# Mixture of experts on Trainium2: the gather and the yield change places between large and small experts, and the last layer norm is shared by three engines

## The reference, cut to what matters

```python
logits = (h @ router).astype(F32)
top_val, top_idx = lax.top_k(logits, TOP_K)            # TOP_K = 2
weights = jax.nn.softmax(top_val, axis=-1)
combine = einsum('blk,blke->ble', weights, one_hot(top_idx, N_EXPERTS))
out = 0
for e in range(N_EXPERTS):                             # 8
    gate, up = jnp.split(h @ w13[e], 2, axis=-1)       # 1024 -> 2 x 3584
    out = out + combine[..., e:e+1] * ((silu(gate) * up) @ w2[e])   # 3584 -> 1024
hx = layer_norm(ALPHA * hx + g2x * out, ln_g, ln_b)    # (256, 1024), mean and variance per token
```

## Time and profile before

| | |
|---|---|
| median of 3 runs | 2219.43 us (2217.98 to 2220.53) |
| the profiled execution, its own time | 2225.52 us |
| its span, first to last instruction | 2223.7 us |
| mean granted clock of TensorE | 0.991 |
| TensorE busy | 2137.1 us, 96% of the span |
| VectorE, ScalarE, GpSimd busy | 1176.0, 915.8, 182.7 us |
| expert stage | about 1308 (first load) to 2210 us |
| one couple, from one to the next at the same place | 217.6 us |
| first large expert: its first low digits, its first product | 1339.40, 1342.88 us |
| last small expert: TensorE's idle time ahead of the first down half of chunk 2 | 1.83 us |
| stores of the result issued | 2216.23 us and about 2220.7 us |

### The profile page before, as it was taken

How to read it: one execution, slowest core, us unless ns; L and a number is a source line. 1 busy time by engine, 2 the same in 40 slices (tenths; PEclk the granted TensorE clock), 3 DMA queues, 4 the chain that set the end, 5 groups by cost and what they waited for, 6 DMA issues and landing times.

```text
span 2223.7 us, 56103 instructions
## 1 busy us (share of the span) xinstructions
PE 2137.1 (96%) x24686; PEld 1580.2 (71%) x24686; DVE 1176.0 (53%) x1581; ACT 915.8 (41%) x1200; POOL 182.7 (8%) x185
## 2 busy tenths in 40 slices
PE   8999999899999989999999999999999899989997
PEld 4677668688888747888888868953895399449843
DVE  3544695522233386666666539820982198129802
ACT  3422013522222185555555437711771277027700
POOL 2100372100000002200000110000000000000000
PEclk8999999999999999999999999999999999999999
DMA  8466406333322351111111249999999999999996
GB/s 294 156 224 236 162 1 189 114 95 94 95 96 98 101 156 35 35 35 35 35 35 59 66 181 347 367 367 407 406 407 401 406 407 407 401 407 407 407 391 274
DMA packets 220597, 491.19 MB, mean 221 GB/s; under 512 B 14631, under 2 KB 107711, under 8 KB 220095
## 3 DMA queue, kind: packets, MB, share of 16 engines
q1 hardware_dynamic: 218974, 482.44, 58.4%
q10 hardware_dynamic: 1442, 6.06, 0.8%
HBM read 486.37 MB, written 2.10 MB: 220 GB/s over the span
## 4 chain that ended last, share of the span: by engine, by line
PE 80%; SPq 5%; DMA 5%; DVE 5%; ACT 3%; issue 2%; POOL 1%; DVEq 0%; ACTq 0%; POOLq 0%
PE bank L1821 13%; PE bank L1852 7%; SPq L935 5%; PE bank L1906 4%; DMA expert_w<-in_moe_w_dram 4%; PE bank L1261 4%; PE bank L1262 4%; PE bank L1263 4%; PE bank L1138 2%; PE bank L1429 2%; PE bank L1167 2%; PE bank L1393 2%; PE bank L1139 2%; PE bank L1140 2%; PE bank L1278 2%
## 5 line engine op out<-in xcount | busy, mean ns | idle before, releaser
L3303 DVE TENSOR_TENSOR w_low<-expert_w,w_high 128x1792 fp32r<-128x1792 f32 (+1 forms) x192 | 383.7, 2023 | 42.1 <-ACT w_high L2470 40.3
L2470 ACT CAST w_high<-expert_w 128x1792 fp32r<-128x1792 f32 (+1 forms) x192 | 325.2, 1701 | 104.7 <-PE bank L1821 72.7
L1906 PE MATMUL bank<-expert_w,arena 128*64 128x448 f32 x1024 | 199.1, 541 | 5.2 <-DMA expert_w<-in_moe_w_dram 5.2
L1906 PEld LDWEIGHTS bank<-expert_w,arena 128*64 128x64 f32 x1024 | 72.2, 137 | 121.6 <-issue 120.2
L1821 PE MATMUL bank<-w_high,xg_high 128*128 128x448 f32 x512 | 146.4, 367 | 7.0 <-DVE xg_low L3293 6.4
L1821 PE MATMUL bank<-w_low,xg_high 128*128 128x448 f32 x512 | 144.9, 364 | 0.0
L1821 PE MATMUL bank<-w_high,xg_low 128*128 128x448 f32 x512 | 144.1, 363 | 0.0
L1261 PE MATMUL bank<-u_high,ring_high 128*128 128x512 f32 x352 | 138.6, 394 | 1.9 <-DVE u_low L2943 1.8
L1262 PE MATMUL bank<-u_low,ring_high 128*128 128x512 f32 x352 | 138.0, 392 | 0.0
L1263 PE MATMUL bank<-u_high,ring_low 128*128 128x512 f32 x352 | 137.7, 391 | 0.0
L2517 ACT ACTIVATE arena<-bank 128x448 f32<-128x448 f32 x16 | 8.7, 545 | 259.9 <-PE bank L1906 259.9
(11 more groups left out here) (458 smaller groups left out, 4191.1 us busy)
## 6 DMA issues: line engine op xcount, KB each, us to landing
expert_w<-in_moe_w_dram SPq DMA_DIRECT2D x128, 1792.0 KB, 19.4
expert_w<-in_moe_w_dram SPq DMA_DIRECT2D x32, 2048.0 KB, 19.4
arena<-in_mod_w_dram SPq DMA_DIRECT2D x48, 1024.0 KB, 8.3
expert_w<-in_moe_w_dram SPq DMA_DIRECT2D x32, 1536.0 KB, 19.2
arena<-in_ffn_w_dram SPq DMA_DIRECT2D x44, 512.0 KB, 5.1
arena<-in_hy_w_in_dram SPq DMA_DIRECT2D x12, 1024.0 KB, 5.3
arena<-in_rw_w_rkv_dram SPq DMA_DIRECT2D x48, 256.0 KB, 2.9
arena<-in_ffn_w_dram SPq DMA_DIRECT2D x11, 1024.0 KB, 4.8
```

What stands on the lines that cost most here:

```text
L1906: last = pe.matmul(b[hd(v), 0:EH], small_x[:, k, :], w[:, kk, v * EH:v * EH + EH], start=(k == 0), stop=(k == KT - 1))
L2470: act.copy(high_piece(kind, n), piece(kind, ering[q % ERN], n // 2, n % 2))\
L3303: dve.tensor_tensor(piece(kind, low[s], n // 2, n % 2), piece(kind, ering[s], n // 2, n % 2), high_piece(kind, n).bitcast(F32), ALU.subtract)\
```

## The change

The gather of a large expert becomes that expert's own first step on TensorE (`large_gathered`), also for the first one, whose special case goes. The yield of a small expert becomes the last step of that small expert on VectorE; the first large expert no longer makes one, and after the loops VectorE waits for the last one and then raises `last_yield`. In the last chunk of a small expert, the second down half of chunk 2 comes behind the turn of chunk 3, and the hidden values of chunk 3 are copied in two steps, so that the first down half waits only for the first. In the last layer norm, ScalarE normalizes the first bank of the first half of the tokens, GpSimd multiplies it by the gain and adds the bias, and VectorE does the rest, in a new order: both halves' statistics first, with the reciprocal and shift for ScalarE between the two statistics of the second half. The first store waits for VectorE and GpSimd (`final0`), the second for VectorE (`final1`).

```diff
@@ -249,12 +249,12 @@
...
     for c in range(EC):
-        pe += ["small_combined"] * (c == 0) + pieces(f"gate{c}") + [f"turned{c - 1}"] * (c > 0) + pieces(f"up{c}")
+        pe += ["large_gathered", "small_combined"] * (c == 0) + pieces(f"gate{c}") + [f"turned{c - 1}"] * (c > 0) + pieces(f"up{c}")
...
         act += ([f"hidden_high{c - 1}"] + pieces(f"high_down{c - 1}")) * (c > 0)
-        dve += ["small_yield"] * (c == 0) + [f"low_gate{c}_0"] + ["xg_low"] * (c == 0)
+        dve += [f"low_gate{c}_0"] + ["xg_low"] * (c == 0)
@@ -271,11 +271,12 @@
...
         pe += pieces(f"small_up{c}", range(2))
-        pe += pieces(f"small_down{c - 1}", range(2)) * (c > 0)
+        pe += pieces(f"small_down{c - 1}", range(2 - (c == last))) * (c > 0)
...
         dve += ["small_pick"] * (c == last) + [f"small_h{c}"]
-    pe += [f"small_turned{last}", "small_gathered"] + pieces(f"small_down{last}", range(2))
-    act += [f"small_hidden{last}"]
+    pe += [f"small_turned{last}", f"small_down{last - 1}_1"] + pieces(f"small_down{last}", range(2))
+    act += [f"small_hidden{last}_0", f"small_hidden{last}_1"]
+    dve += ["small_yield"]
@@ -965,7 +966,7 @@
...
             for tt in range(2):
-                sp.wait_ge(sem("final"), tt + 1)
+                sp.wait_ge(sem(f"final{tt}"), 2 - tt)
@@ -1857,15 +1858,15 @@
...
             pe.wait_ge(sem("tok_taken"), 7)
-            pe.wait_ge(sem("first_expert"), 1)
-            gather(0).then_inc(sem("first_expert"), 1)
             n_passes = pe.alloc_register("n_passes")
-            pe.wait_ge(sem("tok_taken"), 9)
...
                     if c == 0:
-                        step(pe, "expert_vectors", "small_yield", couple)
+                        step(pe, "expert_vectors", "small_pick", couple - 1)
+                        settle(pe)
+                        gather(0).then_inc(sem("expert_products"), 1)
+                        step(pe, "expert_vectors", "small_yield", couple - 1)
@@ -1929,9 +1930,12 @@
...
-            def small_down(c, couple):
-                step(pe, "expert_copies", f"small_hidden{c}", couple)
-                for half in range(2):
+            def small_down(c, couple, halves_=range(2)):
+                for half in halves_:
+                    if c == EC - 1:
+                        step(pe, "expert_copies", f"small_hidden{c}_{half}", couple)
+                    elif half == 0:
+                        step(pe, "expert_copies", f"small_hidden{c}", couple)
@@ -1955,10 +1959,9 @@
...
                     if c:
-                        small_down(c - 1, couple)
+                        small_down(c - 1, couple, range(2 - (c == EC - 1)))
                 small_turn(EC - 1, couple)
-                step(pe, "expert_vectors", "small_pick", couple)
-                gather(0).then_inc(sem("expert_products"), 1)
+                small_down(EC - 2, couple, [1])
@@ -2474,8 +2477,7 @@
...
                     if c == 0:
-                        act.wait_ge(sem("first_expert"), 2)
-                        step(act, "expert_products", "small_gathered", couple - 1)
+                        step(act, "expert_products", "large_gathered", couple)
@@ -2502,9 +2504,13 @@
...
                 act.copy(small_hid[:, 0:3, :].rearrange("p f t -> p (f t)"), low_part[:, 0:3 * SMALL])
-                act.copy(small_hid[:, 4:7, :].rearrange("p f t -> p (f t)"), high_part[:, SMALL:4 * SMALL])
                 act.copy(small_hid[0:SMALL, 3, :], low_part[0:SMALL, 3 * SMALL:4 * SMALL])
-                act.copy(small_hid[SMALL:P, 3, :], high_part[SMALL:P, 0:SMALL]).then_inc(sem("expert_copies"), 1)
+                last = act.copy(small_hid[SMALL:P, 3, :], high_part[SMALL:P, 0:SMALL])
+                if c == EC - 1:
+                    last.then_inc(sem("expert_copies"), 1)
+                    step(act, "expert_products", f"small_down{c - 1}_1", couple)
+                act.copy(small_hid[:, 4:7, :].rearrange("p f t -> p (f t)"), high_part[:, SMALL:4 * SMALL])\
+                    .then_inc(sem("expert_copies"), 1)
@@ -2531,6 +2537,10 @@
...
                 act.activation(stat[:, tt, 2:3], whole[:, tt, 1:2], ACT.Sqrt, bias=eps[:, 0:1]).then_inc(sem("fin_std"), 1)
+                if tt == 0:
+                    act.wait_ge(sem("fin_shift"), 1)
+                    act.activation(XTOK[:, 0, 0:512], bank[0][:, :], ACT.Identity,
+                                   bias=stat[:, 0, 0:1], scale=stat[:, 0, 3:4]).then_inc(sem("fin_scaled"), 1)
@@ -2659,6 +2669,13 @@
...
             last.then_inc(sem("routed"), 1)
+
+            pool.wait_ge(sem("ld_last_rows"), 32)
+            x = XTOK[:, 0, 0:512]
+            pool.wait_ge(sem("fin_scaled"), 1)
+            pool.tensor_tensor(x, x, rowg[:, 0:512], ALU.mult).then_inc(sem("fin_gain"), 1)
+            pool.wait_ge(sem("fin_gain"), 1)
+            pool.tensor_tensor(x, x, rowb[:, 0:512], ALU.add).then_inc(sem("final0"), 1)
@@ -3322,7 +3339,7 @@
...
-            choose(0, slot_no).then_inc(sem("first_expert"), 1)
+            choose(0, slot_no).then_inc(sem("expert_vectors"), len(STEPS["expert_vectors"]) - 1)
@@ -3344,9 +3361,9 @@
...
                                    ALU.subtract))
-            dve.sem_inc(sem("expert_vectors"), len(STEPS["expert_vectors"]))
...
             dve.wait_ge(sem("tok_taken"), 9)
+            dve.sem_inc(sem("expert_vectors"), 1)
@@ -3375,9 +3392,6 @@
...
             def large(couple, item):
-                step(dve, "expert_products", f"small_down{EC - 1}_1", couple - 1)
-                step(dve, "expert_vectors", f"small_h{EC - 1}", couple - 1)
-                yield_small().then_inc(sem("expert_vectors"), 1)
@@ -3423,6 +3437,9 @@
...
                         .then_inc(sem("expert_vectors"), 1)
+                step(dve, "expert_products", f"small_down{EC - 1}_1", couple)
+                step(dve, "expert_vectors", f"small_h{EC - 1}", couple)
+                yield_small().then_inc(sem("expert_vectors"), 1)
@@ -3431,26 +3448,38 @@
...
             passes_made = dve.value_load(passes[0:1, 0:1], min_val=1, max_val=2)
-            step(dve, "expert_products", f"small_down{EC - 1}_1", passes_made * PAIRS - 1)
-            step(dve, "expert_vectors", f"small_h{EC - 1}", passes_made * PAIRS - 1)
-            yield_small().then_inc(sem("last_yield"), 2)
+            step(dve, "expert_vectors", "small_yield", passes_made * PAIRS - 1)
+            dve.sem_inc(sem("last_yield"), 2)
...
                     last = dve.bn_stats(out=halves[:, tt, 6 * half:6 * half + 6], in_=bank[2 * tt + half][:, :])
+                    if (tt, half) == (1, 0):
+                        dve.wait_ge(sem("fin_std"), 1)
+                        link(dve.reciprocal(stat[:, 0, 3:4], stat[:, 0, 2:3]))
+                        dve.scalar_tensor_tensor(out=stat[:, 0, 0:1], in0=whole[:, 0, 0:1], scalar=-1.0, in1=stat[:, 0, 3:4],
+                                                 op0=ALU.mult, op1=ALU.mult).then_inc(sem("fin_shift"), 1)
...
                 dve.wait_ge(sem("fin_var"), tt + 1)
-                for half in range(2):
-                    cs = slice(half * 512, half * 512 + 512)
-                    last = dve.scalar_tensor_tensor(out=XTOK[:, tt, cs], in0=bank[2 * tt + half][:, :],
-                                                    scalar=whole[:, tt, 0:1], in1=rowg[:, cs], op0=ALU.subtract, op1=ALU.mult)
-                dve.wait_ge(sem("fin_std"), tt + 1)
-                link(last)
-                link(dve.reciprocal(stat[:, tt, 3:4], stat[:, tt, 2:3]))
-                dve.scalar_tensor_tensor(out=XTOK[:, tt, :], in0=XTOK[:, tt, :], scalar=stat[:, tt, 3:4], in1=rowb,
-                                         op0=ALU.mult, op1=ALU.add).then_inc(sem("final"), 1)
+
+            def gained(tt, half):
+
+                cs = slice(half * 512, half * 512 + 512)
+                return dve.scalar_tensor_tensor(out=XTOK[:, tt, cs], in0=bank[2 * tt + half][:, :],
+                                                scalar=whole[:, tt, 0:1], in1=rowg[:, cs], op0=ALU.subtract, op1=ALU.mult)
+
+            link(gained(0, 1))
+            dve.scalar_tensor_tensor(out=XTOK[:, 0, 512:D], in0=XTOK[:, 0, 512:D], scalar=stat[:, 0, 3:4], in1=rowb[:, 512:D],
+                                     op0=ALU.mult, op1=ALU.add).then_inc(sem("final0"), 1)
+            for half in range(2):
+                last = gained(1, half)
+            dve.wait_ge(sem("fin_std"), 2)
+            link(last)
+            link(dve.reciprocal(stat[:, 1, 3:4], stat[:, 1, 2:3]))
+            dve.scalar_tensor_tensor(out=XTOK[:, 1, :], in0=XTOK[:, 1, :], scalar=stat[:, 1, 3:4], in1=rowb,
+                                     op0=ALU.mult, op1=ALU.add).then_inc(sem("final1"), 1)
```

## The result

The changed kernel takes **2232.54 us** (median of its seven runs, lowest 2230.17) against 2219.43 before. The ratio is **1.0063**, 95% interval [1.0051, 1.0075]; it leaves out one slow run of each kernel (3396.61 us with a mean clock of 0.58, and 2261.11 us). It is slower by 0.6%, where I had forecast 2217.2 and gave "slower" a chance of 0.05. The profiled execution took 2236.29 us, its span 2234.5 (before: 2225.52 and 2223.7).

What follows compares the result with a forecast made beforehand. After 1470 us the kernel was taken as a weight stream at 407 GB/s, with TensorE setting the pace in the first large expert. Terms -1.3, 0, -1.65, +0.3, +0.4 sum to -2.25: 2217.2 us, range 2214.2 to 2219.9.

Steps and rivals of the forecast that it cites:

- The handovers: From small to next large expert: gather done at 1773.6, wanted at 1774.54, so 0.9 us of cover hides it; term 0.
- The first large expert: At its start: without VectorE's yield, w_low and TensorE start 1.3 us sooner; term -1.3, between -1.35 and -0.55.
- The tail: Last down products: unused gather goes, TensorE waits for landings instead; 1.65 of 3.8 us comes back, bounds -1.2 and -2.0.
- the rival of the falling clock: New TensorE gaps in tail and handovers halve its clock; 3.4 us in the tail, +3.75 in all, 2223.2 us; chance 0.09.
- Loop exit on VectorE: After the loops: 1.5 us of exit work overlaps the yield, last_yield slightly later; term +0.3, between 0 and +0.9.
- Layer norm: At the end: 1.44 us idle after first aggregate, GpSimd slows VectorE; term +0.4, between -0.1 and +1.3.
- The sum: Whole kernel: -1.3 + 0 - 1.65 + 0.3 + 0.4 = -2.25 us, giving 2217.2; chance of the forecast 0.54.

Runs made afterwards that it cites:

- yield_only: The kernel before with only VectorE's yield moved to the end of the small expert: 2217.25 us, ratio 0.9996 [0.9982, 1.0011].
- gather_only: The kernel before with only the gather moved, old tail and old layer norm kept: 2234.5 us, ratio 1.0074 [1.0046, 1.0102].
- pe_unrolled: The changed kernel with TensorE's inner loop over the four couples written out: 2216.37 us, ratio 0.9991 [0.9982, 1.0000].
- combine_first: The changed kernel with the combine put ahead of the gather: 2241.98 us, ratio 1.0103 [1.0088, 1.0118].

## Why the prediction was wrong, point by point

**The handovers: the step that failed.** "The gather [takes] 3.8: done at 1773.6. ScalarE wants it at 1774.54 [...] So 0.9 us of cover hides it. [...] Term 0." The arithmetic took TensorE's stream as gapless from the last down product to the gather. Between them stands the loop's own edge. It is in no view that I had read: the page counts no branch as busy, and I looked at the earlier trace rows for VectorE's loop exit but never at the same line on TensorE, for which the view of the kernel before has the 6096 ns. I even had a mark of it in a row, the 2.27 us of idle time before the combine in the earlier trace rows, put down to VectorE's yield, and believed the name. There the yield ended at 1990.80 and the branch at 1991.04, 0.2 us apart, and the combine started at 1991.41; at the third large expert it was 1773.17, 1773.40 and 1773.77. With the branch in, the sum would have been 1773.4 + 3.8 = 1777.2 at full clock and no second gap, 2.7 us late each time; the second fetch (a gap of 1.55 to 2.33 us) and the half clock make it 6.4 to 7.5. The other half of the step, "each us of lateness would cost a us of TensorE, and less in the stream", held: 18.4 us went into the time for 21.0 of lateness.

**The first large expert: right.** The timeline of its start, answering to the earlier trace rows:

```profile
1330.12 3.81 PE L1795 MATMUL bank<-arena 128*128 128x128 f32 x32 [0.23 <-DVE arena L3305]
...
1334.04 2.03 DVE L3320 TENSOR_TENSOR w_low<-expert_w,w_high 128x1792 fp32r<-128x1792 f32 x1 [0.99 <-ACT w_high L2473]
...
1337.39 0.67 PE L1822 MATMUL bank<-w_high,xg_high 128*128 128x448 f32 x2 [1.55 <-DVE xg_low L3310]
```

From the gather's start to the first product 7.27 us instead of 8.76 (1342.88 less 1334.12): -1.5, forecast -1.3. In yield_only it is 7.27 as well and in gather_only 8.70, so this belongs to the yield; entering the loop cost the gather nothing.

**The tail: the mechanism right, the size not.** TensorE's and VectorE's lines, answering to the earlier trace rows:

```profile
2206.01 2.79 PE L1944 MATMUL bank<-expert_w,arena 128*64 128x512 f32 x12
...
2210.76 7.92 PE L1944 MATMUL bank<-expert_w,arena 128*64 128x512 f32 x28 [1.96 <-DMA expert_w<-in_moe_w_dram]
...
2218.82 1.51 DVE L3380 SCALAR_TENSOR_TENSOR arena<-bank,arena 64x512 f32<-64x512 f32 x2 [18.14 <-PE bank L1944]
```

The gather is gone and a wait for the landing has come, as forecast. But after that wait of 2 us the clock falls to 0.50 (the window from 2212 to 2214), and the 28 products take 7.92 us instead of 6.23. From their start, which follows the last landing but one, to the yield it is 8.06 us, where the forecast has 6.70 (2200.2 + 0.15 to 2207.05). It is 8.05 in pe_unrolled, and 6.77 in gather_only (2206.91 to 2213.68), where the clock stayed at 1.00. So 1.4 of the 1.65 us went to the clock, and about -0.3 is left. This is the rival of the falling clock, in the place it named and at less than its price (1.4 us for 3.4). The wait alone does not explain it. In this same execution, ahead of the second large expert, the same products stand behind a wait as long and are through in 6.60 us, with the clock at 1.00:

```profile
1538.95 6.60 PE L1944 MATMUL bank<-expert_w,arena 128*64 128x512 f32 x28 [1.98 <-DMA expert_w<-in_moe_w_dram]
```

What decides between the two stays open. My argument against the rival, that gaps of 1.8 us stood in small experts at clock 1.00, was true and no protection.

**Loop exit on VectorE:** from the yield's start to the first statistics 3.02 us instead of 2.93, +0.1 for +0.3. **Layer norm:** the timeline, VectorE's lines and GpSimd's second product, answering to the earlier trace rows.

```profile
2221.84 1.30 DVE L3457 BATCH_NORM_STATS2 arena<-bank 128x6 f32<-128x512 f32 x2 [1.51 <-PE bank L1979]
...
2224.81 0.70 DVE L3457 BATCH_NORM_STATS2 arena<-bank 128x6 f32<-128x512 f32 x1 [1.43 <-PE bank L1979]
...
2227.44 1.09 DVE L3474 SCALAR_TENSOR_TENSOR arena<-arena 128x512 f32<-128x512 f32 x1
2228.06 1.60 POOL L2678 TENSOR_TENSOR arena<-arena 128x512 f32<-128x512 f32 x1
...
2230.15 1.28 DVE L3481 SCALAR_TENSOR_TENSOR arena<-arena 128x1024 f32<-128x1024 f32 x1
```

9.59 us from the first statistics to the end instead of 9.05: +0.54 for +0.4. The idle 1.43 us stand where they were forecast. The half with both inputs in SBUF took 1.09 us beside GpSimd, which is 0.4 over the 0.68 of the earlier trace rows, where I took 0.2 and the rule of the Trainium skill ("SBUF — State Buffer", section "Who interferes with whom") gave an estimate of 0.3; and GpSimd's second product beside it took 1.60 for 1.28. Both pay, which is what mutual exclusion would look like; no run here tests it. GpSimd is done at 2229.66, before VectorE.

**The sum:** the parts that I costed come to -1.5 - 0.3 + 0.1 + 0.5 = -1.2 us. The kernel in which the branch is out of the way, pe_unrolled, has 2216.37 us beside 2218.84, -2.5 us with an interval from -4.0 to 0. That holds both this sum and the forecast of -2.25, and cannot tell either from no change; that it lies so near the forecast is luck in part, since the head start came out 0.2 better and the tail 1.4 worse. The term that I called nothing was worth 15 us (+13.1 in place of -2.25).

## What to carry to other kernels

A step moved across the end of a loop moves across that loop's branch. Look up what the branch takes on that engine's sequencer before costing the move: on TensorE here it was 6.1 us, over a hundred times the same instruction on ScalarE and VectorE, and it had been free only because nothing behind it was wanted. "Idle before" with an engine's name against it is not proof: check that the named instruction ended when the wait did. And where work is taken out of a place that feeds TensorE between two transfers, the gap that opens can halve its clock for the products that follow: in the tail it did so in five of seven kernels.

## What the runs showed that I had not expected

- A backward branch of TensorE takes 6.00 to 6.26 us in each kernel with that loop unhinted, 0.46 to 0.51 with a prefetch hint of 0.04 us, and 0.08 when it falls through. With the loop written out, the kernel before is no slower (0.9991 [0.9981, 1.0001]).
- Behind such a branch, 34 instructions in, TensorE stood still again until 5.7 to 6.0 us after the branch's end, since the loop's head was that close to the end of a block. Putting the head at a block's start was worth 7 us of 2232 by the medians.
- The last 28 down products stood behind a wait of 1.68 to 2.15 us in seven kernels. In five of them the clock went down to 0.50 on the way and they took 7.92 or 7.93 us; in the other two, gather_only (1.68 us) and combine_first (1.99 us), it stayed at 1.00 and they took 6.62 and 6.57. So the length of the wait alone does not decide it.
- The shared layer norm takes 9.59 us in the first order and 8.26 in the second, against 9.05 on VectorE alone: whether sharing helped at all hung on what VectorE did while it waited for TensorE.
